# A copy, a mix, an exponential and two waits moved in a two-layer hybrid decoding step

## What is computed

```python
def _layer(x, pos0, past_rows, win_rows, s0, lb, norm_g, w_in, ...):
    h = _rms(x, norm_g)
    (hq, hf, hi, hgate, dq, dk, dv, iq, ik, iw, dgate, nq, ..., ma, mb, mc) = _split(h @ w_in, IN_SPLITS)
    ho, s_new = _hgrn2(hqa, hk, hv, logf, s0)                  # gated linear recurrence
    yb = _dsa_attend(dq_h, iq_h, iw, qpos, keys, values, fik)  # the 256 keys with the best index scores
    o_cs = _nsa_cmp_sel(nq_h, qpos, ck, cv, sk, sv)            # compressed keys, and the best blocks of 64
    o_w = _window_attend(nq_h, qpos, wk, wv, ...)              # the last 512 tokens
    o_c = gb[..., 0:1] * o_cs[:, :, 0] + gb[..., 1:2] * o_cs[:, :, 1] + gb[..., 2:3] * o_w
    gates = jax.nn.sigmoid(jnp.stack([ma, mb, mc], axis=2))
    m = jnp.sum(gates * jnp.einsum('blnc,ncd->blnd', ys, w_branch), axis=2)
    return x + m @ w_out, rows, wfull[:, -min(WINDOW, lw):], s_new

# in _dsa_attend
    dots = jnp.einsum('bthd,bsd->bths', iqb, ik) * IDX_DIM ** -0.5
    score = jnp.einsum('bth,bths->bts', iwb, jax.nn.relu(dots))
    sel = lax.top_k(score, n_top)[1]
```

## Time and profile before

| | |
|---|---|
| executions, us | 982.62, 976.34, 980.28 |
| profiled execution: span, us | 979.2 |
| mean granted TensorE clock | 0.988 |
| TensorE matmul busy, us | 943.2 (96%) |
| VectorE, ScalarE, GpSimd busy, us | 484.9, 304.5, 132.5 |
| moved by DMA, MB | 188.98, mean 193 GB/s |

### The profile page before, as it was taken

The page is one execution under the profiler, slowest core; times in us unless marked ns, Lnnn a source line. Parts: engine busy times, 40 slices in busy tenths (PEclk is TensorE's granted clock), DMA queues, the critical chain, the costliest instruction groups (busy, mean ns, idle before and its releaser), DMA issues.

```text
span 979.2 us, 17076 instructions
## 1 busy us (share of the span) xinstructions
PE 943.2 (96%) x6248; PEld 760.6 (78%) x6248; DVE 484.9 (50%) x1374; ACT 304.5 (31%) x659; POOL 132.5 (14%) x258
## 2 busy tenths in 40 slices
PE   9999999899999998999999999998999999899998
PEld 7888778777777776888888886787676867678887
DVE  4224548778643674134240345697785546731331
ACT  2135432247633113310121363331576311223000
POOL 0510000002032360000060000000020413600000
PEclk9999999999999999999999999999999999999999
DMA  7644417434199696334453435263342988952432
GB/s 266 203 157 162 165 54 332 178 140 173 44 332 386 215 385 225 135 129 139 163 182 139 146 135 200 108 286 129 146 162 86 373 306 310 378 173 89 162 140 87
DMA packets 56501, 188.98 MB, mean 193 GB/s; under 512 B 9186, under 2 KB 22882, under 8 KB 43874
## 3 DMA queue, kind: packets, MB, share of 16 engines
q1 hardware_dynamic: 43138, 138.56, 40.3%
q0 software_dynamic: 12992, 49.16, 13.2%
q10 hardware_dynamic: 288, 0.18, 0.1%
HBM read 177.47 MB, written 18.77 MB: 200 GB/s over the span
## 4 chain that ended last, share of the span: by engine, by line
PE 85%; DMA 5%; DVE 4%; ACT 3%; issue 1%; DVEq 1%; ACTq 1%
PE ps L868 22%; PE ps L998 17%; PE ps L1344 9%; DMA slab<-in_weights_dram 5%; PE ps L1237 5%; PE ps L1357 3%; PE ps L1351 3%; PE ps L880 3%; PE ps L893 2%; PE ps L1315 2%; PE ps L1148 2%; PE ps L1136 2%; PE ps L857 1%; PE ps L1216 1%; PE ps L1116 1%
## 5 line engine op out<-in xcount | busy, mean ns | idle before, releaser
L868 PE MATMUL ps<-hT,slab 128*128 128x264 f32 (+1 forms) x1184 | 274.9, 391 | 6.8 <-DMA slab<-in_weights_dram 5.9
L868 PEld LDWEIGHTS ps<-hT,slab 128*128 128x128 f32 (+1 forms) x1184 | 224.7, 192 | 47.2 <-DMA slab<-in_weights_dram 6.2
L998 PE MATMUL ps<-hT,slab 128*128 128x264 f32 x768 | 186.1, 400 | 1.7 <-DVEq L2109 1.7
L998 PEld LDWEIGHTS ps<-hT,slab 128*128 128x128 f32 x768 | 147.7, 196 | 34.5 <-DVEq L2037 3.2
L1369 ACT ACTIVATE arena<-ps 128x512 f32<-128x512 f32 (+21 forms) x152 | 69.8, 484 | 187.9 <-PE ps L868 66.7
L1344 PE MATMUL ps<-Y,slab 128*128 128x264 f32 x384 | 85.8, 386 | 0.0
L1344 PEld LDWEIGHTS ps<-Y,slab 128*128 128x128 f32 x384 | 73.0, 190 | 12.5
L1237 PEld LDWEIGHTS ps<-arena,w 128*128 128x128 f32 x512 | 58.4, 192 | 10.0 <-issue 6.6
L1763 DVE SCALAR_TENSOR_TENSOR arena<-arena,small 128x264 f32<-128x264 f32 x26 | 11.0, 488 | 110.1 <-ACT arena L1444 110.1
L1237 PE MATMUL ps<-arena,w 128*128 128x128 f32 x512 | 61.4, 278 | 0.0
L593 POOL DMA_DIRECT2D arena<-in_pages_kv_dram x64 | 33.3, 520 | 160.8 <-DVEq L2273 123.9
(11 more groups left out here) (365 smaller groups left out, 1208.8 us busy)
## 6 DMA issues: line engine op xcount, KB each, us to landing
slab<-in_weights_dram SPq DMA_DIRECT2D x86, 1024.0 KB, 5.0
arena<-in_pages_kv_dram SPq DMA_DIRECT2D x64, 256.0 KB, 8.3
arena<-in_pages_kv_dram POOLq DMA_DIRECT2D x64, 256.0 KB, 6.7
arena<-in_pages_kv_dram POOLq DMA_DIRECT2D x64, 128.0 KB, 7.8
arena<-in_pages_kv_dram SPq DMA_DIRECT2D x64, 128.0 KB, 10.3
out_dram<-in_state_win_dram POOLq DMA_DIRECT2D x2, 4088.0 KB, 29.4
arena<-in_state_hgrn_dram SPq DMA_DIRECT2D x2, 2048.0 KB, 27.9
out_dram<-arena POOLq DMA_DIRECT2D x2, 2048.0 KB, 7.3
```

Of the source, the lines that this page charges most:

```text
L868: last = mm(ps[0:job[3], n % 2, 0:LT], v[:, k, job[2]:job[2] + job[3]], hT[:, k, :], start=(k == 0), stop=(k == KD - 1))
L998: last = mm(ps[:, bank, 0:LT], v[:, k, (d % 2) * 128:(d % 2) * 128 + 128], hT[:, k, :], start=(k == 0), stop=(k == KD - 1))
```

## The change

The edits; all but the last are in both layers:

- POOL's copy of the sliding rows waits for the third index dot (`dot 2`) instead of the recurrence's level step `a 0`.
- TensorE's waits for ScalarE's steps "iw" and "new" ahead of hq1, and for the last `relu` ahead of `key_scores(1)`, are taken out. Later waits on the same engine imply them.
- `mix(6)` (mix 17) stands ahead of the wait for "left out", with its own wait for "c 2".
- ScalarE's exponential of the sliding window and its sum stand right behind that of the compressed keys, and VectorE's reciprocal, scaling and own-key product of it behind "n cmp".
- In the product of the new tokens' values the two loops are exchanged, so that the column strip changes with every product.
- One more filler product at the start: `keep_busy(5, 5)`.

```diff
-                     + ["hid 2", "c 2", "scores", "hb 3", "hid 3", "c 3", "e cmp", "t cmp", "e w", "e", "PT"])
+                     + ["hid 2", "c 2", "scores", "hb 3", "hid 3", "c 3", "e cmp", "e w", "t cmp", "e", "PT"])
...
-                pool.wait_ge(hg_p.sem, hg_p(l, "a 0"))
+                pool.wait_ge(pidx_p.sem, pidx_p(l, "dot 2"))
                 pool.dma_start(s_win[l1].rearrange("a s w c -> (a s) w c"),
...
             pe.wait_ge(idle_set, 1)
-            keep_busy(5, 4)
+            keep_busy(5, 5)
...
-                pe.wait_ge(pidx_a.sem, pidx_a(l, "iw"))
-                pe.wait_ge(sidx_a.sem, sidx_a(l, "new"))
                 project("hq1", 0)
                 dots(2)
                 dots(3)
...
                 dots(6)
                 dots(7)
-                pe.wait_ge(pidx_a.sem, pidx_a(l, f"relu {NH - 1}"))
                 key_scores(1)
...
+                pe.wait_ge(dc_a.sem, dc_a(l, "c 2"))
+                mix(6)
                 pe.wait_ge(sidx_v.sem, sidx_v(l, "left out"))
                 mm(ps[0:ROWS, 5, 32:33], K("seq_rows")[eight[3]], dropped[eight[3], NQ:NQ + 1], start=True, stop=True)
-                pe.wait_ge(dc_a.sem, dc_a(l, "c 2"))
-                mix(6)
                 pe.wait_ge(dc_a.sem, dc_a(l, "scores"))
...
-                for b in range(NS):
-                    for a in range(3):
+                for a in range(3):
+                    for b in range(NS):
                         mm(ps[eight[b % 4], 4 * (b // 4) + a, 0:128], pn8[:, a * ROWS + b * NH:a * ROWS + (b + 1) * NH], vn[:, a, :],
                            start=True, stop=False)
...
                 act.drain().then_inc(dc_a.sem, dc_a.mark("e cmp"))
+                A(SW[0:ROWS, 0:WIN + 1], SW[0:ROWS, 0:WIN + 1], ACT.Exp, bias=st[0:ROWS, 44:45], accum_out=sa[0:ROWS, 44:45])
+                act.drain().then_inc(dc_a.sem, dc_a.mark("e w"))
                 take(6)
...
                 act.wait_ge(dc_v.sem, dc_v(l, "masked"))
-                A(SW[0:ROWS, 0:WIN + 1], SW[0:ROWS, 0:WIN + 1], ACT.Exp, bias=st[0:ROWS, 44:45], accum_out=sa[0:ROWS, 44:45])
-                act.drain().then_inc(dc_a.sem, dc_a.mark("e w"))
                 A(SS[:, 0:PAST + 1], SS[:, 0:PAST + 1], ACT.Exp, bias=st[:, 43:44], accum_out=sa[:, 43:44])
...
                 TS(c4, c4, c40, None, ALU.mult).then_inc(dc_v.sem, dc_v.mark("n cmp"))
+                ve.wait_ge(dc_a.sem, dc_a(l, "e w"))
+                nc.vector.reciprocal(st[0:ROWS, 47:48], sa[0:ROWS, 44:45])
+                ve.drain()
+                TS(SW[0:ROWS, 0:WIN + 1], SW[0:ROWS, 0:WIN + 1], st[0:ROWS, 47:48], None, ALU.mult)
+                ve.drain()
+                TS(dw, own[0:ROWS], SW[0:ROWS, WIN:WIN + 1], None, ALU.mult)
                 ve.wait_ge(dc_a.sem, dc_a(l, "t cmp"))
```

More of the change, by code:

```diff
@@ L2207, in _ @@
                 ve.drain().then_inc(dc_v.sem, dc_v.mark("masked"))
[L2208 to L2211, removed]
                 ve.wait_ge(dc_a.sem, dc_a(l, "e"))
@@ L2217, in _ @@
                 TS(dn, own, SS[:, PAST:PAST + 1], None, ALU.mult)
-                TS(dw, own[0:ROWS], SW[0:ROWS, WIN:WIN + 1], None, ALU.mult)
                 ve.drain().then_inc(dc_v.sem, dc_v.mark("new p"))
```

## The result

The changed kernel takes 970.57 us (median of 20 runs, 966.29 to 978.88), the kernel before 979.05 us (20 runs, 975.64 to 984.36). The ratio is 0.9916 with an interval of 0.9895 to 0.9937: 8.5 us faster, where 18.5 were forecast. The profiled execution of the changed kernel has a span of 967.2 us, 12.0 less than before.

What follows compares the result with a forecast made beforehand. TensorE's own stream, busy 943.2 of 979.2 us, was taken as the bound. Terms -9.0 - 6.1 + 0.6 - 1.6 - 2.0 - 0.4 = -18.5 gave a 960.7 us span; with the median 1.1 above, 962 us, range 956.5 to 971.

Steps and rivals of the forecast that it cites:

- the left-out waits: TensorE's waits for VectorE at line 1267, once a layer: mix ahead of them saves 9.0 us over two layers.
- the slabs: TensorE's waits for a weight slab held by the copy, ahead of a projection: moving the copy earlier saves 6.1 us.
- The copy and the keys: At key_scores(3): removed index waits and keys delayed by the moved copy together cost +0.6 us over two layers.
- the same paragraph's upper bound: At key_scores(3): with a 29 us copy, 5.3 us idle and 1.7 us slow clock per layer, +14.0 us.
- the two index waits: TensorE's idle ahead of hq1 and key_scores(1): removal in itself saves 1.43 us a layer, 2.9 in all.
- Rival 1: Index keys slip through beside the copy and the removed index waits give 2.9 us: 958.5 us, chance 0.2.
- The order of the loops: At line 1306: changing column strip with every product saves 2.0 us over two layers, bounds 0 and that.
- Rival 3: Mix goes ahead, but TensorE's clock falls around the two short waits that follow: 965 us, chance 0.1.
- The exponential: Sliding-window exponential moved under mix 18, cutting TensorE's wait at line 1297: -1.6 us, bounds 0 and -1.7.
- the filler: Fifth filler product at the start, keeping TensorE going ahead of line 893: -0.4 us, between +0.1 and -1.4.

Runs made afterwards that it cites:

- copy_only: Kernel before with only the sliding-rows copy issued behind the third index dot, both index waits kept: 975.34 us, ratio 0.9963.
- cs_waits_back: copy_spill with the two index waits put back: 962.59 us, ratio 0.9807 to the kernel before.
- copy_dot7: Changed kernel with the sliding-rows copy issued behind the eighth index dot instead of the third: 962.68 us, ratio 0.9822 to the kernel before.
- copy_spill: Changed kernel with the copy behind the eighth index dot and SP's spill load behind the second half of the value products: 957.81 us, ratio 0.978.
- loops_only: Kernel before with only the two loops of the 48 small products exchanged: 982.79 us, ratio 1.005.
- mix_only: Kernel before with only mix(6) moved ahead of the wait for "left out": 974.39 us, ratio 0.994.
- undo_copy: Changed kernel with the sliding-rows copy back at level step a 0: 970.61 us, ratio 0.9905 to the kernel before.

## Why the prediction was wrong

The forecast of 962 us stood 8.6 us under the median of 970.57. Of its 18.5 us, 3.4 at the left-out waits and 3.3 at the slabs were clock, the other 11.8 idle time: by span times clock 966.7 - 11.8 = 954.9, and a clock of 0.995 instead of 0.988. Measured were 960.8 and 0.992. So some 6 us are idle time, lost in the two places that follow, and some 3 us are clock.

**The copy and the keys: the mechanism right, the term mis-sized.** "So while the copy runs, what SP's queue has asked for waits for its end" holds: keys 20.9 us, and a slab issued at 122.5 took 21.6. The estimate of 24 us for the copy was 24.2, and the keys' landing, given as 142.6, was 142.35. That the landing was hit is partly luck: the start's 1.3 us had moved the copy, issued at 117.1 instead of 118.1, along with TensorE, which was at key_scores(3) at 139.53. The failing step is "key_scores(3) then stands at 142.29 - 1.43 = 140.86 [...] 1.7 us of idle, and +0.3 us against before". Counted from the copy's issue, TensorE came 0.3 us sooner than forecast and the keys 0.75 later (the copy 0.2 longer, the keys 1.05 us behind its end instead of 0.5), so that 1.7 us became 2.82; and the step priced the wait without its clock, for which the same paragraph's upper bound has 1.7 us. The term of +0.6 us came out as +5.9 in the profile, as much as the slab's -5.7, which was right (forecast -6.1). What TensorE wins between the copy's issue and the keys' reader turns into idle time: the second index wait, 0.95 us, is about what the key wait of layer 0 gains on copy_only's (2.82 and 1.83). What is won ahead of the issue moves the copy too (119.1 in copy_only, 117.1 here). Of the 2.9 us of the two index waits, some 3 where nothing is held (cs_waits_back), the longer key waits took back 2.5. Rival 1, keys not held, was given 958.5 us. copy_dot7, in which they are not, has 962.68; copy_spill, without the issue waits as well, 957.81.

**The order of the loops: the step "bounds 0 and that" failed.** The products did take 1.49 us, forecast 1.4. The lower bound of nothing was wrong: the exchange alone makes the kernel 0.5% slower, since, by the packets' times, it brings TensorE's instruction loads some 0.7 us closer to the spill load (0.6 in loops_only), so that the next one stands behind it. Neither DMA stood in the argument. In the kernel before, a wait called issue of 0.32 us stood in the same products, and I hadn't asked where it came from. The Trainium skill, "Runtime: NRT & Kernel Launch", section on instruction fetch mechanics, says that an engine's instructions come in 16 KiB blocks by a DMA queue of the engine's own and that this is mostly hidden. The trace agrees on the blocks (0.80 MB in 49 packets), and not on the hiding in this place: waits of 2.79 and 2.49 us.

**The left-out wait: the idle time right, the clock's share not.** The step is "So each of these two waits costs its length and some 1.7 us on top". In the profiled run the place gave 9.8 us, forecast 9.0. But by itself (mix_only) the part gives 5.9 us, 3.5 to 8.2, nearly all of it idle time. The clock's slow stretch wasn't the wait's own: without the wait it came behind waits of 0.81 and 0.62 us that are left, or elsewhere. Nor did every longer wait bring one: behind 2.49 us in the changed kernel and behind 1.83 us in copy_only the products ran at full clock (3.72 us for a mix, 1.93 for the 64 products). Rival 3 had this, at 0.1.

**The rest.** The exponential (-2.0 in the profile, forecast -1.6) and the filler (-1.3, forecast -0.4, bound -1.4) were somewhat better than forecast, and of what the changed profile would show every wait was there; the one wait that exceeds its bounds is the keys' in layer 1, 3.09 us. What I had not listed, the two issue waits, is 5.3 us. That queues take turns on a DMA engine packet by packet, as the Trainium skill states ("DMA: Bandwidth & Descriptors", section on queues, rings and completion order), did not keep the hold short: key loads took up to 20.9 us beside the copy and 2.1 in the median without it. The prediction left room for this with "very long packets", and the trace shows the copy in packets of 65 KB, an estimated 2.7 us of an engine each. So turns and a long hold don't exclude each other here; which of them it was, the trace doesn't show.

Still open is why the clock falls in one run of the same kernel more often than in the next (0.983 to 0.995), and with that how much of a removed wait's clock is won for good. No run here tells it.

## What to carry to other kernels

When a long DMA is moved, list each small load that is still to land when it starts, and the time at which its reader comes after the change, not before; the cure was to issue the copy some 7 us later (124.4 instead of 117.1), behind the last of these loads, and it was worth 9 us by the ratios, 4.8 of them idle time. In a stretch of many very short products look at the instruction queue too, and keep a large transfer from starting in it: one moved wait on SP gave 7.6 us, 4.3 of them idle time. Judge an idle time that is removed by its length alone, treat the clock it seems to cost as a possible extra, and compare kernels by span times granted clock beside the medians.

## What the runs showed of the hardware

By the times of the instruction packets, TensorE can stand still for its own instructions: among products of 29 ns it used up a 16 KB block in some 3.5 us, and with 1,056 KB on the DMA engines it then waited 2.1 to 2.8 us for the next (changed kernel, undo_copy, copy_dot7, loops_only). Beside a DRAM-to-DRAM copy of 4,088 KB in packets of 65 KB, a 32 KB load took up to 20.9 us instead of 2.1 and a slab 21.6 instead of 5.0. And the clock's share of the scatter is large: 12.6 us between runs of one kernel, of which 3 us are left when each span is multiplied by its granted clock.
